# Key selection of two gathered token tiles moved out of the gate groups, and the one-hot matrices made by one vector instruction

## The reference, cut to what matters

```python
def peer(h, w_pq, sub_keys, expert_u, expert_v):
    ...
    qh = (t @ w_pq).reshape(T, PEER_HEADS, 2, D_HALF)
    scores = jnp.einsum('thpd,hpkd->thpk', qh, sub_keys)
    s_top, i_top = lax.top_k(scores, PEER_TOPK)
    cand = s_top[:, :, 0, :, None] + s_top[:, :, 1, None, :]
    cand_idx = i_top[:, :, 0, :, None] * N_KEYS + i_top[:, :, 1, None, :]
    best, pos = lax.top_k(cand.reshape(T, PEER_HEADS, -1), PEER_TOPK)
    idx = jnp.take_along_axis(cand_idx..., pos, axis=-1)
    gate = jax.nn.softmax(best, axis=-1)
    # per token: sum over its 8 x 16 chosen experts of gate * gelu(t . expert_u[e]) * expert_v[e]
```

## Time and profile before

| | |
|---|---|
| time, median of 3 runs | 4180.6 us (4178.39 to 4185.6) |
| the profiled execution | 4183.85 us, its span 4182.1 us |
| PE busy | 3948.3 us, 94% of the span |
| DVE busy | 2458.2 us, 59% |
| ACT busy | 604.4 us, 14% |
| POOL busy | 1747.4 us, 42% |
| DMA | 1024.62 MB, 245 GB/s over the span |
| gate groups, by layer | 627.80 to 781.74 and 2675.89 to 2829.79 us |
| steps, by layer | 781.74 to about 2112 and 2829.79 to about 4160 us |

### The profile page before, as it was taken

The page is one execution under the profiler, slowest core; times in us unless marked ns, Lnnn a source line. Parts: engine busy times, 40 slices in busy tenths (PEclk is TensorE's granted clock), DMA queues, the critical chain, the costliest instruction groups (busy, mean ns, idle before and its releaser), DMA issues. The chain is left out here.

```text
span 4182.1 us, 40852 instructions
## 1 busy us (share of the span) xinstructions
PE 3948.3 (94%) x13330; PEld 2194.4 (52%) x13330; DVE 2458.2 (59%) x5173; ACT 604.4 (14%) x1276; POOL 1747.4 (42%) x1419
## 2 busy tenths in 40 slices
PE   7999996899999999999979999869999999999997
PEld 3455575554555555555544456755455555555553
DVE  3424599766555555555554257996555556555556
ACT  2212216300000000000011121471000000000000
POOL 0011047375545545545301100773655545555542
PEclk9999999999999999999989999999999999999999
DMA  8801205689989999989740020176999999989994
GB/s 325 312 17 47 91 11 136 174 324 376 340 330 344 342 331 342 341 325 342 266 153 0 36 106 11 57 172 182 408 342 342 334 338 346 333 331 344 339 331 177
DMA packets 494251, 1024.62 MB, mean 245 GB/s; under 512 B 228960, under 2 KB 265888, under 8 KB 493344
## 3 DMA queue, kind: packets, MB, share of 16 engines
q0 software_dynamic: 147456, 536.94, 34.3%
q1 hardware_dynamic: 346272, 486.04, 33.7%
q10 hardware_dynamic: 384, 0.09, 0.0%
HBM read 968.90 MB, written 54.04 MB: 245 GB/s over the span
## 5 line engine op out<-in xcount | busy, mean ns | idle before, releaser
L1407 PE MATMUL ps<-big,y_nat 128*128 128x384 f32 x4096 | 1363.3, 486 | 3.4 <-ACT kn_area L1489 3.1
L1407 PEld LDWEIGHTS ps<-big,y_nat 128*128 128x128 f32 x4096 | 777.6, 190 | 601.1 <-issue 122.2
L1857 POOL DMA_INDIRECT big<-in_peer_v,gates_area x512 | 616.0, 1203 | 676.4 <-DVE big L1742 560.6
L1847 POOL DMA_INDIRECT big<-in_peer_u,gates_area x512 | 677.6, 1323 | 485.2 <-DVE kn_area L1727 350.4
L1415 PE MATMUL ps<-y_nat,gates_area 128*128 128x512 f32 x1536 | 685.2, 596 | 13.8 <-DVE gates_area L1697 13.8
L1742 DVE SCALAR_TENSOR_TENSOR big<-big,kn_area 128x1024 f32<-128x1024 f32 x512 | 657.2, 1284 | 61.8 <-DMA big<-in_peer_v,gates_area 41.1
L1415 PE MATMUL ps<-big,gates_area 128*128 128x512 f32 x1536 | 680.1, 592 | 0.0
L1727 DVE CUSTOM_DVE_ANT_0 big<-big,y_nat 128x1024 f32<-128x1024 f32 x512 | 597.1, 1220 | 22.1 <-DMA big<-in_peer_u,gates_area 21.7
L1415 PEld LDWEIGHTS ps<-y_nat,gates_area 128*128 128x128 f32 x1536 | 293.7, 191 | 357.9 <-issue 310.0
L1415 PEld LDWEIGHTS ps<-big,gates_area 128*128 128x128 f32 x1536 | 292.0, 190 | 339.9 <-issue 306.0
L1496 ACT ACTIVATE gates_area<-ps 128x384 f32<-128x384 f32 x256 | 125.5, 490 | 2252.2 <-PE ps L1407 2252.1
(11 more groups left out here) (269 smaller groups left out, 2877.1 us busy)
## 6 DMA issues: line engine op xcount, KB each, us to landing
y_nat<-in_peer_ut SPq DMA_DIRECT2D x256, 512.0 KB, 7.4
y_nat<-in_peer_v SPq DMA_DIRECT2D x128, 512.0 KB, 4.9
big<-in_peer_v SPq DMA_DIRECT2D x128, 512.0 KB, 6.0
big<-in_w_mod SPq DMA_DIRECT2D x24, 2048.0 KB, 10.8
expert_gates<-big SPq DMA_DIRECT2D x10, 4096.0 KB, 20.8
gates_area<-expert_gates SPq DMA_DIRECT2D x126, 192.0 KB, 8.3
kn_area<-expert_gates SPq DMA_DIRECT2D x126, 192.0 KB, 9.2
big<-in_w_in SPq DMA_DIRECT2D x8, 2048.0 KB, 16.0
```

Of the source, the lines that this page charges most:

```text
L1407: last = pe.matmul(ps[:, 6 + par, 0:ND], u_s[par][:, k, :], h_t[:, k, 0:ND], start=(k == 0), stop=(k == KD - 1))
L1847: pool.indirect_dma_start(out=u_ring[:, k, :], out_offset=None, in_=io["peer_u"][:, :], in_offset=bass.IndirectOffsetOnAxis(ap=exp_idx[:, ...
L1857: pool.indirect_dma_start(out=v_ring[:, k % VSLOTS, :], out_offset=None, in_=io["peer_v"][:, :], in_offset=bass.IndirectOffsetOnAxis(ap=ex ...
```

## The change

The one-hot matrices of a group now lie in one buffer `hot` (two key halves x eight tokens), and one DVE tensor_tensor of 128x2048 makes all sixteen unscaled. ACT scales the first three of the first half (`BY_SCALAR`), and POOL scales the other five in place with one tensor_tensor of 128x640, for which it now waits on DVE. Nothing of the key selection is left in the groups.

Tile 3's keys are selected by DVE alone: heads 0 to 2 after the last group, heads 3 to 7 in steps 0 to 2, its best pairs in steps 3 and 4, its key numbers in steps 5 and 6 by a new function `keys_of_slots` (16 scalar_tensor_tensor with outputs 16 words apart, and one reduce), which also replaces POOL's multiply. Tile 4 does the same during steps 8 to 51, beside the gathering of tile 3. For this ACT copies tile 4's scores once into `h_t`'s free columns (128x2048), ahead of the exponential of the dense softmax. Tile 3's loop on DVE is written out (60 steps) and no longer a loop of 2 x 30. POOL adds tile 4's pairs between heads 2 and 4 of tile 3, and waits for tile 4's choice ahead of head 7. The softmax of each gathered tile and ACT's exponential for it stand at the start of its own steps. The load of the final norm weights (`fw`) moves behind SP's loop, since its buffer serves as scratch. `wst` and `normw` become two halves of one buffer `mixw`, which is scratch too.

```diff
         gate_s = carve(big, 5120, N_KEYS, P)
-        hot1 = carve(big, 21504, 2, OCT, P)
-        hot2 = carve(big, 21504 + 2 * OCT * P, 2, OCT, P)
+        hot = carve(big, 21504, 2, 2, OCT * P)
...
-                    if final:
-                        sp.dma_start(fw, io["final_norm_w"].broadcast_to([P, D])).then_inc(s_in, 16)
...
-                    sp.wait_ge(s_kb, 1)
+                    sp.wait_ge(s_sbe, 2 * PH + 1)
                     v0()
...
-                        pe.wait_ge(s_oh, 4 * (n + 1))
-                        pe.wait_ge(s_am, 4 * (n + 1))
-                        pe.wait_ge(s_oh2, 2 * (n + 1))
+                        pe.wait_ge(s_oh, n + 1)
+                        pe.wait_ge(s_am, BY_SCALAR * (n + 1))
+                        pe.wait_ge(s_oh2, n + 1)
...
+                    act.wait_ge(s_sbe, 2 * PH)
+                    act.activation(sc_4, sc_b[:, 1, :, :].rearrange("p (k a) b -> p k (a b)", a=2), ACT.Copy).then_inc(s_sbe, 1)
                     act.wait_ge(s_b7, 1)
                     act.activation(exp_gate[:, 0:DENSE, :], gate_xa, ACT.Exp).then_inc(s_e7, 1)
...
-                        act.wait_ge(s_oh, 4 * n + 1)
-                        for tt in range(4):
+                        act.wait_ge(s_oh, n + 1)
+                        for tt in range(BY_SCALAR):
...
+                    def keys_of_slots(rank, x, keys, eq, dst, h0, h1):
+
+                        v = keys.rearrange("p t (h x) a -> p (t h) x a", x=2)
+                        n = (h1 - h0) * TOPK
+                        for a in range(TOPK):
+                            lane.do(dve.scalar_tensor_tensor(
+                                out=eq[:, 0:n * TOPK].rearrange("p (h k a) -> p h k a", k=TOPK, a=TOPK)[:, :, :, a],
+                                in0=rank[:, 0, h0 * TOPK:h1 * TOPK].rearrange("p (h k) -> p h k", k=TOPK), scalar=float(a),
+                                in1=v[:, h0:h1, x, a:a + 1].broadcast_to([P, h1 - h0, TOPK]), op0=ALU.is_equal, op1=ALU.mult))
+                        lane.settle()
+                        lane.do(dve.tensor_reduce(dst[:, h0 * TOPK:h1 * TOPK], eq[:, 0:n * TOPK].rearrange("p (s a) -> p s a", a=TOPK),
+                                                  AX.X, ALU.add))
+                        lane.settle()
...
-                        dve.tensor_tensor(hot1[:, n % 2, 0:4, :], iota_k[:, :].unsqueeze(1).broadcast_to([P, 4, N_KEYS]),
-                                          choice_t[:, i % 2, OCT * g:OCT * g + 4].unsqueeze(2).broadcast_to([P, 4, N_KEYS]),
-                                          ALU.is_equal).then_inc(s_oh, 1)
-                        dve.tensor_tensor(hot2[:, n % 2, :, :], iota_k[:, :].unsqueeze(1).broadcast_to([P, OCT, N_KEYS]),
-                                          choice_t[:, i % 2, P + OCT * g:P + OCT * (g + 1)].unsqueeze(2).broadcast_to([P, OCT, N_KEYS]),
-                                          ALU.is_equal).then_inc(s_oh, 1)
-                        for tt in range(4, OCT - 2):
-                            t = OCT * g + tt
-                            dve.tensor_scalar(hot1[:, n % 2, tt, :], iota_k[:, :], choice_t[:, i % 2, t:t + 1],
-                                              choice_t[:, i % 2, 2 * P + t:2 * P + t + 1], ALU.is_equal, ALU.mult).then_inc(s_oh, 1)
...
+                        both_choices = choice_t[:, i % 2, 0:2 * P].rearrange("p (x t) -> p x t", x=2)[:, :, OCT * g:OCT * (g + 1)]
+                        dve.tensor_tensor(hot[:, n % 2, :, :].rearrange("p x (t k) -> p x t k", k=N_KEYS),
+                                          iota_k[:, :].unsqueeze(1).unsqueeze(1).broadcast_to([P, 2, OCT, N_KEYS]),
+                                          both_choices.unsqueeze(3).broadcast_to([P, 2, OCT, N_KEYS]), ALU.is_equal).then_inc(s_oh, 1)
...
+                    for h in range(3):
+                        first_half(h, top_3, index_3, src_3(h), dst_3)
+                        second_half(h, top_3, index_3, dst_3)
                     dve.wait_ge(s_f, GROUPS)
                     for j in range(EARLY):
                         weigh(j, j % 2, j // 2, j - 1 if j >= 2 else None)
...
+                        if j == 5:
+                            keys_of_slots(rowf_3, 0, keys_3, eq_3, exp_i1[:, G0, :], 0, PH)
+                        if j == 6:
+                            keys_of_slots(colf_3, 1, keys_3, eq_3, exp_i2[:, G0, :], 0, PH)
+                            expert_rows(G0, flat_3)
...
+                    def choose_next(s):
+
+                        if s < 2 * PH:
+                            if s % 2 == 0:
+                                first_half(s // 2, top_4, index_4, src_4(s // 2), dst_4)
+                            else:
+                                second_half(s // 2, top_4, index_4, dst_4)
+                        if 26 <= s < 26 + PH:
+                            best_pairs(s - 26, 2 * PH + s - 25, CTX, cand_4, cut2_4, pos_4)
...
+                        if s in (36, 38):
+                            keys_of_slots(rowf_4, 0, keys_4, eq_4, exp_i1[:, CTX, :], 2 * (s - 36), 2 * (s - 36) + 4)
+                        if s in (40, 42):
+                            keys_of_slots(colf_4, 1, keys_4, eq_4, exp_i2[:, CTX, :], 2 * (s - 40), 2 * (s - 40) + 4)
...
-                        for tt in range(OCT - 2, OCT):
-                            t = OCT * g + tt
-                            pool.tensor_scalar(hot1[:, n % 2, tt, :], iota_k[:, :], choice_t[:, i % 2, t:t + 1],
-                                               choice_t[:, i % 2, 2 * P + t:2 * P + t + 1], ALU.is_equal, ALU.mult).then_inc(s_oh2, 1)
-                    pool.wait_ge(s_kb, 1)
+                        v = hot[:, n % 2, 0, BY_SCALAR * P:OCT * P].rearrange("p (t k) -> p t k", k=N_KEYS)
+                        at = 2 * P + OCT * g
+                        pool.wait_ge(s_oh, n + 1)
+                        pool.tensor_tensor(v, v, choice_t[:, i % 2, at + BY_SCALAR:at + OCT].unsqueeze(2).broadcast_to([P, OCT - BY_SCALAR, N_KEYS]),
+                                           ALU.mult).then_inc(s_oh2, 1)
```

179 lines of the change are left out of this document (99 added, 80 removed).

## The result

The changed kernel takes 4233.91 us in the median of four runs (4228.77 to 4251.57), the kernel before 4183.1 in the same comparison (4178.39 to 4198.42). The ratio is 1.0123 with a 95% interval of 1.0107 to 1.0139, so about 51 us slower. The profiled execution is the slowest of the four, 4251.57 us, with a span of 4249.4 us.

The account below looks back on a forecast made before the run. DVE was taken to set the pace in the gate groups, PE in the steps. 4183.85 + 113.0 + 3.6 - 18.4 = 4282.05, less 3.25 to the median: 4279 us; range 4185 to 4340.

Parts of the forecast that it names:

- the collision: Gate groups: DVE's compare and POOL's multiply, each with two SBUF inputs, cannot overlap; 2.21 + 1.25 = 3.46 us a group.
- the forecast's pattern: Gate groups: two compares back to back, then two multiplies; 8.0 us a pair at full clock; chance 0.56.
- turns: Rival in the gate groups: compare and multiply alternate, 3.4 us a group, total 4192, said as 4200; chance 0.22.
- gate groups, two layers: Time added by the gate group stages: 210.4 against 153.9 us, +56.5 a layer, +113.0 in all.
- entry, two layers: Ahead of the dense softmax: ACT's copy of 2048 elements delays the exponential by 1.8 us, +3.6 for two layers.
- stalls at the start of gathering: Steps: gathering starts 11 us earlier, so PE's 13.8 us of waiting and 4.6 of slow products go, -18.4.
- Durations: Gate group operations: compare of 2048 elements 2.29 us, POOL's multiply of 640 elements 1.25; at the entry, ACT's copy 1.8.
- free overlap: Rival in the gate groups: compare and multiply run together, 2.95 us a group, total 4150; chance 0.15.
- Who goes first: Gate groups: DVE issues its next compare before POOL's multiply, and this order keeps itself up, 4.0 us a group.
- The pair's price: Two gate groups: 8.0 us, plus 1.86 in one pair of three for the lower clock, so 8.62 on average.
- The chain: Gate groups: one buffer passes through DVE, POOL and PE in 5.9 us; with two buffers at least 2.95 a group.
- late step: Steps: DVE's added selection work for tile 4 might not be hidden in a few steps, up to +10 us.

Follow-up runs that it names:

- run 1: The changed kernel measured again with no edit: median 4234.34 us, ratio 1.0128 to the kernel before.
- run 2: The changed kernel with DVE's compare reading the choices from PSUM instead of SBUF: median 4159.29 us, ratio 0.9944.
- run 6: The changed kernel with three buffers instead of two for the one-hots and their PSUM banks, choices still in SBUF: median 4183.49 us, ratio 1.0002.
- run 4: The changed kernel with only DVE's wait for the next tile's choices four groups earlier: median 4230.58 us.
- run 8: The changed kernel with both DVE's and POOL's waits for the next tile's choices four groups earlier: median 4228.07 us.
- run 5: The kernel before with only the new one-hots, key selection staying in the gate groups: median 4223.82 us, ratio 1.0097.
- run 3: The kernel before with only the key selection moved out of the gate groups, one-hots as before: median 4151.01 us, ratio 0.9918.

## Why the prediction was right or wrong

The direction came from a mechanism that the runs confirm, the collision. The size did not come from the forecast's pattern: 68 of 96 groups in the first trace and 74 in run 1 ran in turns, the rival that had been given 0.22. That the measured 4234 lies in the range of 4185 to 4340 is owed to a range that took in both patterns, and so is in part luck.

| step of the sum | forecast | measured |
|---|---|---|
| gate groups, two layers | +113.0 | +66.0 in the first trace, +63.5 in run 1 |
| entry, two layers | +3.6 | +3.9 (2.64 against 0.69 of waiting, twice) |
| stalls at the start of gathering | -18.4 | -17.3 in run 1 |
| total | +98.2 | +51 (medians) |

- **Durations: right.** The compare 2.29 forecast and 2.28 to 2.29 measured, the multiply 1.25 and 1.25, the copy 1.8 and 1.91. The trace of before was enough to price operations it did not contain.
- **The collision: right, and shown** by run 2, in which one operand's place removes it. The Trainium skill ("SBUF — State Buffer", section "SBUF: two separate sides") has the pair of ports as an exclusive lock when DVE's instruction has two SBUF inputs and GpSimd's reads SBUF; the trace agrees, with 3.38 us for the compare in turns against 2.29 with its choices in PSUM. The other side, *free overlap* at 4150 (which the prediction's paragraph on the skill means by "the last rival"), describes the kernel of run 2, with 4159, and not this one. What the prediction overdrew is "a group needs both in turn". By run 6 a collision costs 0.97 of the multiply's 1.25 us, in turns 1.11 and the handover.
- **Who goes first: the step that failed.** The sum rested on "the pattern keeps itself up". It does only while the second group's products end before POOL can start its multiply, that is within the compare beside them and the handover, 2.29 + 0.15 = 2.44 us. At the full clock they take 1.75. Where enough of them runs at the lower level they end later, POOL's multiply gets in between, and turns begin. The first pair of layer 0 shows it:

```profile
635.65 6.69 PE L1401 MATMUL ps<-big 128*128 128x128 f32 x32 [6.38 <-POOL big L1888]
...
639.43 2.29 DVE L1709 TENSOR_TENSOR big<-iota_k,gates_area 128x2048 f32<-128x2048 f32 x1 [5.05 <-PE ps L1401]
...
641.87 1.25 POOL L1888 TENSOR_TENSOR big<-big,gates_area 128x640 f32<-128x640 f32 x1 [5.15 <-DVE big L1709]
642.37 2.90 DVE L1709 TENSOR_TENSOR big<-iota_k,gates_area 128x2048 f32<-128x2048 f32 x1 [0.65 <-PE ps L1401]
```

PE's 32 matmuls take 6.69 us and end at 642.34. The compare of 639.43 has ended at 641.72 by then, and POOL starts at 641.87, 0.5 us before DVE may go on. The same is seen behind 691.55, where the second group's products take 2.64 us, and not behind 750.12, where 3.29 of the 5.44 us belong to the first group and only 2.15 to the second: there the pairs went on. The traces of the changed kernel and of runs 1, 4 and 8 hold 43 pairs with groups behind them. In 20 the second group's products ended 1.75 to 2.40 us after the next compare had started, and each was followed by a pair; in 23 it was 2.45 to 2.97 us, with a granted clock of 0.73 or less in them, and each was followed by turns. So the slow clock, which I had priced only as an addition to pairs, is what ends them. Turns in their turn keep up until something costs POOL its 0.02 us (runs 4 and 8). So both patterns occur in each execution of this kernel that was profiled, in shares that vary from run to run: 28 of 96 groups in pairs in the first trace, 22 in run 1.
- **The pair's price: right only in the long stretch, and there by two misses that cancel.** In layer 0 from 759.52 to 810.91 the pairs take 7.92 and 9.2 us in alternation, 8.56 in the mean, against 8.62. I had taken one pair in three on the lower clock at 1.86 us more; it was every second, at some 1.3 more. In run 1 none of the 11 pairs ran at the full clock throughout: the 32 matmuls of each took 5.43 to 6.36 us instead of 3.81, and the pairs 8.4 to 9.9 us, 9.2 in the mean. The Trainium skill's loop in "TensorE: Matmul & The Clock Gate", section "HAM oscillation — how this bites in real kernels", in which every burst starts slow, is not what the rows of the long stretch show, with every second burst at 3.81 us; run 1, in which every burst has a part at the lower level, is nearer to it.
- **Turns: under-priced.** I put 3.4 us on a group and 167.1 on the stage. A group takes 3.545, and a stage in turns throughout takes 174.6 (run 5). The period was taken below the sum of 2.21 and 1.25, with nothing for DVE's handover to POOL, which is 0.15 and is paid in every group. With 3.545 the same sum, 47 * 3.545 + 7.3 a layer, gives 4206 instead of 4192 (and the 4225 given for a multiply of 1.54 us should have been about 4219, by 94 * 0.29 more). The measured time lies between this and the forecast, as the mixture of patterns would have it.
- **The chain: right.** 5.9 us were forecast for one buffer, and it is 6.00 in run 2. The handover from DVE to POOL was 0.14 and from POOL to PE 0.26, not 0.1 each; that from PE to DVE was 0.03.
- **The stalls: right.** 1343.0 us from the first score of layer 1 to the end in run 1, against 1352.3 before, 9.3 less; in layer 0 8.0 less, when the copy is taken out. The gathering starts 74.1 us behind the first step (forecast 73), released by a late store. Of PE's 13.8 us of waiting for `weigh` nothing is left in run 1. No late step came up either.
- **What the prediction did not see:** the halves of the change do not add. Against before, the selection alone gives -32 us (run 3) and the one-hots alone +41 (run 5); together they are +51, not +9. Where DVE has to wait 1.11 us for POOL in every group, its selection is hidden, and moving it frees nothing. Run 5 has no pair in any of its 96 groups, and stages of 174.6 us against 182 to 191 in the changed kernel; that the selection keeps DVE behind POOL at the contested moments is the likely reason, but was not tested by itself. So on top of the new one-hots the move costs 22 us of pairs (63.5 - 41.4, by the stages) and 3.9 us at the entry, and wins 17.3 us of stalls, which is the 9 us between run 5 and the changed kernel.

What stays open: the cause of the loss of 15 us in layer 1 of the first trace. It came once in the traces taken, with PE waiting for its own instructions. Nothing was tried on it. Open too is what decides how many pairs follow at groups 16 and 32: the stretches at the lower clock fell differently in each execution.

## What to carry to other kernels

When an operation is handed from VectorE to GpSimd, look at where its inputs lie before looking at its length: two inputs in SBUF on VectorE beside GpSimd made a sum out of what the queues show as parallel, and reading one operand from PSUM, where it lay anyway, was worth 75 us. Ask of every saving on an engine whether that engine will wait for another in its place; work that sits in such a wait is free, and moving it away gives nothing. And where two engines compete for each turn, work out both orders and what switches between them, for the time can be a mixture; here a third buffer removed the worse one and was worth 51 us.

## What the runs showed of the hardware

- The order at a contested port was decided by 0.02 to 0.03 us. One wait more in POOL's queue, already satisfied, tipped it, and tipped it at the places where this wait stood (runs 4 and 8); the same wait in DVE's queue alone did not (run 4). The Trainium skill says that issue order and not the shape of the operation decides who blocks ("SBUF — State Buffer", section "Who interferes with whom"); the trace agrees, with 645.42 against 645.44.
- Such a lead was lost at fixed places and in most cases came back after one to four pairs.
- By the Trainium skill ("SBUF — State Buffer", section "SBUF: two separate sides") the ports are held for the whole instruction. The traces show a little less: of POOL's 1.25 us DVE is held for 1.11 in turns, and a collision costs 0.97 with both queues full (run 6).
- A compare of 128x2048 with one input in PSUM takes 2.29 us, the same as with both in SBUF (run 2).
- Idle spans of some 4 us between bursts of 3.8 us of matmuls brought the granted clock to the lower level for most of the first group of every second burst in the long stretch of layer 0, in a steady sequence of 7.92 and 9.2 us; in run 1 it was part of every burst. Once turns had begun, their gaps of 1.5 us between 2.0 us of matmuls left the matmuls at 2.02 us.
